# Order of the first loads and the first weight splits in a two-block transformer kernel

## What is computed

```python
def hybrid_layer(x, w_in, ...):
    h = rms_norm(x, g_pre)
    a_q, a_kv, a_g, b_cq, b_ckv, b_kr, c_q, c_kv, z = split_cols(h @ w_in)
    o_a = nsa_attention(..., rel_bias[:NSA_HEADS])      # compressed, selected and window branches
    o_b = causal_block_attention(q_full, k_full, ...)   # queries and keys with rope
    o_c = banded_attention(..., rel_bias[NSA_HEADS:], sinks)
    mixed = concatenate([o_a, o_b, o_c]) * silu(z)
    return x + rms_norm(mixed @ w_out, g_post)

def t5_bucket(dist): ...    # bias = rel_bias[:, t5_bucket(dist)], masked where dist is out of the window
```

## Time and profile before

| | |
|---|---|
| median of three runs | 2542.4 us (2539.15 to 2543.17) |
| the profiled execution | 2540.47 us |
| its span in the profile | 2538.7 us |
| mean granted TensorE clock | 0.984 of full speed |
| TensorE busy | 2440.3 us, 96% of the span |
| VectorE, ScalarE, POOL busy | 1290.7, 659.1, 655.7 us |
| read from DRAM | 219.05 MB, 89 GB/s over the span |

### The profile page before, as it was taken

How to read it: one execution, slowest core, us unless ns; L and a number is a source line. 1 busy time by engine, 2 the same in 40 slices (tenths; PEclk the granted TensorE clock), 3 DMA queues, 4 the chain that set the end, 5 groups by cost and what they waited for, 6 DMA issues and landing times. The chain is left out here.

```text
span 2538.7 us, 34867 instructions
## 1 busy us (share of the span) xinstructions
PE 2440.3 (96%) x13142; PEld 1958.2 (77%) x13142; DVE 1290.7 (51%) x1918; ACT 659.1 (26%) x1331; POOL 655.7 (26%) x510
## 2 busy tenths in 40 slices
PE   8999899997999999998999998999999998999997
PEld 6776677665888887886888886888887886888886
DVE  5557465656433345877433344333345877433344
ACT  3037331462111102543211102111102543211101
POOL 2016410372333212003333212333212003333211
PEclk9999999998999999999999998999999999999999
DMA  6220232102222322212222331222322312222322
GB/s 252 67 96 18 67 123 68 41 2 74 99 99 97 110 94 72 96 40 83 91 99 93 115 101 52 99 92 98 116 91 67 100 44 83 83 99 97 119 91 78
DMA packets 58088, 222.70 MB, mean 88 GB/s; under 512 B 6340, under 2 KB 8532, under 8 KB 57724
## 3 DMA queue, kind: packets, MB, share of 16 engines
q1 hardware_dynamic: 53712, 206.87, 24.3%
q10 hardware_dynamic: 4268, 14.33, 1.5%
HBM read 219.05 MB, written 5.80 MB: 89 GB/s over the span
## 5 line engine op out<-in xcount | busy, mean ns | idle before, releaser
L180 DVE CAST two_hi<-two_raw 128x1024 fp32r<-128x1024 f32 (+1 forms) x292 | 220.0, 753 | 903.3 <-PE bank L249 890.7
L242 PE MATMUL bank<-xh,two_hi 128*128 128x512 f32 x1728 | 429.7, 391 | 0.1
L249 PE MATMUL bank<-xl,two_hi 128*128 128x512 f32 x1728 | 428.5, 390 | 0.0
L245 PE MATMUL bank<-xh,two_lo 128*128 128x512 f32 x1728 | 426.8, 389 | 0.0
L182 DVE TENSOR_TENSOR two_lo<-two_raw,two_hi 128x1024 fp32r<-128x1024 f32 (+1 forms) x292 | 401.0, 1373 | 10.0
L249 PEld LDWEIGHTS bank<-xl,two_hi 128*128 128x128 f32 x1728 | 324.9, 188 | 67.6
L245 PEld LDWEIGHTS bank<-xh,two_lo 128*128 128x128 f32 x1728 | 324.3, 188 | 67.5
L242 PEld LDWEIGHTS bank<-xh,two_hi 128*128 128x128 f32 x1728 | 323.0, 188 | 68.4 <-issue 1.2
L1617 POOL TENSOR_TENSOR hm<-sg,hm 128x512 f32<-128x512 f32 x88 | 197.6, 2245 | 559.3 <-ACT hm L1599 559.3
L242 PE MATMUL bank<-hh,two_hi 128*128 128x512 f32 x704 | 171.8, 392 | 0.0
L249 PE MATMUL bank<-hl,two_hi 128*128 128x512 f32 x704 | 171.4, 390 | 0.0
(11 more groups left out here) (276 smaller groups left out, 2951.2 us busy)
## 6 DMA issues: line engine op xcount, KB each, us to landing
two_raw<-in_up SPq DMA_DIRECT2D x180, 512.0 KB, 3.3
two_raw<-in_down SPq DMA_DIRECT2D x64, 704.0 KB, 4.0
one_raw<-in_w_in SPq DMA_DIRECT2D x44, 512.0 KB, 3.4
two_raw<-in_w_in SPq DMA_DIRECT2D x40, 512.0 KB, 3.3
one_raw<-in_w_out SPq DMA_DIRECT2D x16, 512.0 KB, 3.4
two_raw<-in_w_out SPq DMA_DIRECT2D x16, 512.0 KB, 3.4
w<-in_w ACTq DMA_DIRECT2D x2, 2048.0 KB, 18.4
x<-in_x SPq DMA_DIRECT2D x4, 512.0 KB, 6.5
```

The source lines that it names most:

```text
L180: v.tensor_copy(st.hi[:, h, 0:w], st.raw[:, r, 0:w]).then_inc(st.hi_made, 1)
L242: pe.matmul(out[:], st.hi[:, slot, k * P:(k + 1) * P], xh[:, h * kp + k, :], start=h == 0 and k == 0, stop=False)
L245: pe.matmul(out[:], st.lo[:, slot, k * P:(k + 1) * P], xh[:, h * kp + k, :], start=False, stop=False)
L249: mm = pe.matmul(out[:], st.hi[:, slot, k * P:(k + 1) * P], xl[:, h * kp + k, :], start=False, stop=h == pieces - 1 and k == kp - 1)
```

## The change

The four small inputs of the bias are no longer asked for by SyncE ahead of everything, but by ScalarE as the first thing it does, ahead of its table load. SyncE begins with the gains and x. VectorE splits the first two weight tiles at the end of its own start, ahead of the mask additions, instead of at the beginning of the layer. What is computed is the same.

```diff
     def sync(sp):
-        for dst, src in ((first.rel, "rel"), (first.hot, "hot"), (first.msk, "msk"), (first.msk_near, "msk_near")):
-            sp.dma_start(dst[:], d[src]).then_inc(s["loaded"], 16)
         sp.dma_start(kit.gains, d["gains"]).then_inc(s["gains_in"], 16)
...
     def scalar(a):
+        for dst, src in ((first.rel, "rel"), (first.hot, "hot"), (first.msk, "msk"), (first.msk_near, "msk_near")):
+            a.dma_start(dst[:], d[src]).then_inc(s["loaded"], 16)
         a.preload_act_table_set(EXP_LN)
...
         v.memset(kit.ones[:], 1.0).then_inc(s["set"], 1)
+        for n in range(HL_RING):
+            split_first(v, st, n)
         mask_rows(v)
...
-        if l == 0:
-            for i in range(HL_RING):
-                split(i)
         for i in range(N_IN):
             if i < N_IN - HL_RING:
                 split(i + HL_RING)
```

## The result

| | before | after |
|---|---|---|
| median | 2541.8 us (16 runs, 2537.99 to 2545.08) | 2548.15 us (16 runs, 2546.53 to 2553.24) |
| ratio, 95% interval | 1 | 1.0026 (1.0019 to 1.0033) |
| profiled execution, its span | 2540.47, 2538.7 us | 2547.35, 2545.6 us |

The loss is 0.26%, just above the 0.2% that a measurement of this kernel can tell from no change. The forecast was 2545.6 us with a range of 2540 to 2550.5. The direction and the mechanism came out and the time lies in the range, but the size does not fit the forecast case: 6.3 us more where 4.2 were forecast, with bounds of 1.5 and 5.1. That size belongs to rival 1, which had a chance of 0.20.

What follows compares the result with a forecast made beforehand. TensorE's matmul stream, busy 96% of the span, was taken to bound the kernel. A 2.7 us later compression plus 1.5 of clock gave 4.2 more: 2544.7 or 2546.6, middle 2545.6 us, range 2540 to 2550.5.

Steps and rivals of the forecast that it cites:

- the forecast case: Whole kernel: start gain turns into idle time before the compression; 4.2 us more (+1.5 to +5.1), chance 0.50.
- rival 1: Before the compression: s1 at 61.5 and the clock's whole 4 us together cost 8.3 us, 2550; chance 0.20.
- The stream starts at 13.3: TensorE's start: splits ahead of masks let the unbroken stream begin at 13.3 instead of 16.54, gain 3.2 us.
- The rival of the displaced x: At the start: small inputs displace x, stream at 14.9, masks 1.6 later, s1 at 61.5, 2547.5 us; chance 0.06.
- The small inputs are delayed by 0 to 2 us: Bias products at the start: begun at 4.35 before, delayed 0 to 2 us, ending between 9.2 and 11.2, hidden.
- The masks push the copies 1.4 us back, to 17.5: VectorE's masks end at 15.2 instead of 9.78, so ScalarE's bias copies are issued at 17.5 instead of 16.18.
- s1 lands at 59.9: ScalarE's queue: later copies put s1 at 58.6, one raw tile's 1.26 us makes 59.9, between 57.5 and 61.5.
- The chain behind s1 takes 9.87 us: VectorE's work after s1 ends at 69.8, so the compression starts 2.7 us later, after 6.3 us idle.
- The issues of s1 and w1 end near 40 and 41, and the evictions stay at about 42.5: ScalarE's reciprocal root behind the blocked issues keeps the evictions at about 42.5; hidden from TensorE.
- The clock costs 1.5 us, of at most 4: The idle time before the compression lowers TensorE's clock: 1.5 us extra, bounds 0 to 4.
- Rival 2: Nothing lost at s1: undisturbed splits give 2541.8 us, s1 early altogether 2538.8; chance 0.24 in both forms.
- The sum: Whole kernel: 2.7 us later compression plus 1.5 us of clock, 4.2 us more.

Runs made afterwards that it cites:

- the first experiment: On the changed kernel, ScalarE asks for s1 and w1 ahead of the two bias copies instead of behind them; 2536.1 us, ratio to before 0.9976.
- the splits alone: Changed kernel with the four small inputs put back first on SyncE's queue, first two splits still ahead of the masks; 2547.95 us, ratio 1.0023.
- the two with dummies: Changed kernel with 26 or 34 dummy matmuls on TensorE ahead of the compression; 2543.5 us (ratio 1.0001) and 2540.7 us (0.9995).
- the two last versions: The first experiment plus POOL waiting for the first two splits, 2533.8 us; or with inputs back on SyncE and two raw tiles ahead of x, 2533.1 us.

## Why the prediction came out as it did, point by point

- *The stream starts at 13.3.* It started at 14.39. The split durations were right (2.90 and 3.97 us against 2.88 and 3.96). The thought that split 0 could end 1 us sooner had no room in it: the 2.88 already holds a quick first cast (0.67 us). What it says of the cast came out: begun at 7.54, just ahead of POOL's first subtraction at 7.62, it took 0.69; in the first experiment, begun at 7.43 with POOL at work from 7.23, it took 1.61. The landing was mis-sized: I moved it by the 1.64 us of the issues and kept the time in flight, but x took 4.9 instead of 4.1 us and the first raw tile 5.8 instead of 4.9. The rival of the displaced x had this in it, at 1.64; it was 0.9. The slow first stretch (spacing of 0.43 us) moved along, from 22.6 to 20.5; that it is the lower level is read from the spacing alone, for the granted clock in the profile is 1.00 there. It does not always move along: in the splits alone, begun at 14.90, L469 came at 26.83, a whole us ahead of the changed kernel's.
- *The small inputs are delayed by 0 to 2 us.* The bound was wrong: bias products began at 7.84 instead of 4.35, 3.5 us later. It stayed hidden as the step said: they ended at 12.69, ahead of the second split's 14.34.
- *The masks push the copies 1.4 us back, to 17.5.* They came at 18.00, 1.8 us back: the last mask ended 0.8 us later than forecast, with the split ahead of it, and the way of the stores took 2.0 us (16.0 to 18.0) where 2.3 were forecast. The doubt that 16.18 could be ScalarE's own place in its program is settled by the runs with `s1` moved: in them ScalarE asked for `s1` at that place at 13.94 and, in the kernel before, at 14.71. It was the stores that held the copies.
- *s1 lands at 59.9.* 61.68, outside the bounds given for it (57.5 to 61.5). From the copy's issue it took 43.7 us instead of 41.04. The step took one raw tile of 1.26 us in the way of the copies; 2.6 us were added. The share of the 19 to 27 us stretch is 0.73 instead of 0.54: `k1` and two raw tiles now run there. That they are the cause is argued and not shown, and a part may be chance: the kernel before's two further profiles took 41.7 and 42.0 us, the splits alone 42.95, the two with dummies 43.7 and 43.4. The upper end of that term, 1.5 us on top of the tile, was nearer than the value taken.
- *The chain behind s1 takes 9.87 us.* 61.68 to 71.49, 9.81: right, and so was the conclusion that the gain turns into idle time. That the idle time came out so close (6.45 us, forecast 6.3) is luck: TensorE was ready 1.6 us later than forecast and the compression began 1.7 later. The reading behind it was off as well: the 0.42 us was idle time of the weight loads, and the matmuls had none. With the 5.86 us that L469's start is ahead of the compression where nothing waits, they were ready at 66.97 and not at 66.72.
- *The issues of s1 and w1 end near 40 and 41, and the evictions stay at about 42.5.* They ended at 41.98 and 44.32, and the root came at 44.37. TensorE did not wait for it here; in the splits alone it did, 0.80 us at 51.19, for a split that came late behind the evictions.
- *The clock costs 1.5 us, of at most 4.* 3.3: from 4.40 us at the compression's start to 7.74 at L1124, 2.84 in the compression and 0.5 behind it. The upper bound for the compression, 2.9 by the ratio of the weight loads, was the right value. I took the lower end because of a compression in which the clock fell only at its end; the one that matters begins at the lower clock.
- *Rival 1* is what happened in kind, at 7.7 of its 8.3 us in the profile. *Rival 2*, nothing lost at `s1`, was made true in its second form by the first experiment (2536.1, forecast 2538.8). Its first form left out the clock: by its own numbers TensorE would have been ready at 66.72 - 5.5 = 61.2 and idle until 66.5.
- *The sum.* It was 4.2; in the profiles it is 6.9, with 1.7 of the miss in `s1` (with the landing of x), 1.8 in the clock, and 0.8 given back by the end.

One thing in the reading was too strong: "level" was said of one execution. The row of 0.42 us looked like a harmless wait and was one draw of a wait of the weight loads between 0.4 and 2.5 us, with 4 us hanging on it.

## What to carry to other kernels

A change that starts the main engine earlier is worth what the next late arrival lets through: before counting the gain, follow each queue that a delayed store or copy feeds and see what small, late-needed load stands at its end. Here moving one load ahead of two bulk copies was worth 12 us in the changed kernel and 2.8 in the kernel before, and the reordering at the start paid only with it: from 2538.85 us (the kernel before with `s1` moved) to 2536.1 with the change as it is, and to 2533.1 to 2533.8 with the two last versions (medians; the first of these steps alone is not clear of noise, for the intervals of its two ratios overlap). And a wait of TensorE ahead of thin products is priced with the clock: let it come early and idle, and it can lose more than by coming late.

## What the runs showed of the hardware

- Thin products pay the lower clock nearly in full: 32 matmuls of 31 columns took 3.66 us at the upper level and 7.03 at the lower, 1.9 times.
- With 1.47 us of idle time ahead of them the compression ran slow (6.40 us), with none it did not (3.66), though in the first TensorE had done 26 full matmuls just before the gap. With no idle time it was still 4.19 us in the profile with the raw tiles first, where the clock fell at 64.7, during the last third of it.
- Two copies that keep only about 8 and 4 of 16 DMA engines busy (shares of 0.54 and 0.25) hold up everything behind them in their queue: in the changed kernel the issue of `s1` itself took 17.40 us, and with `w1`'s it kept ScalarE's next instruction, needed for all evictions, until 44.37; VectorE waited 4.89 us for it, which stayed hidden.
- VectorE and POOL beside each other: a cast 1.75 instead of 0.69 us, a subtraction 2.18 instead of 1.23, POOL's eight subtractions 12.8 instead of 10.0. The Trainium skill's page SBUF — State Buffer (SBUF: two separate sides) describes an exclusive lock of a shared port pair; the run with POOL waiting agrees, with the short times on both engines (1.23 and 10.00 us).
